# First inputs of a two-block network on one core: stage 0 of the parameter rows loaded and turned ahead of the others, x turned and split by quarters, its squares summed per token on ScalarE

## The reference

```python
hn = rmsnorm(h, norm_mix_g)            # y = x * rsqrt(mean(x*x) + eps), times the gain
proj = hn @ w_in + b_in                # 2048 x 13320
(q, k, v, o_pre, i_pre, f_pre, cb, cc, ch, gm_pre, gc_pre) = split(proj)
hm = mlstm_chunkwise(q, k, v, i_pre, f_pre)      # four heads, gates from i_pre, f_pre
```

## Time and profile before

| | us |
|---|---|
| three timed runs, median | 2799.66 |
| lowest, highest | 2789.32, 2804.08 |
| the profiled execution, its time | 2790.9 |
| its span (first to last instruction) | 2789.0 |
| TensorE busy in it | 2721.1 |
| VectorE, ScalarE busy | 1709.8, 1296.5 |

### The profile page before, as it was taken

One profiled execution on the slowest core, in us unless ns is written; L12 is line 12 of the kernel. 1 busy time (PEld: TensorE's weight loads), 2 busy tenths in 40 slices (PEclk: granted clock), 3 DMA queues, 4 the chain that ended last, 5 costly groups with the idle time before them and its releaser, 6 DMA issues.

```text
span 2789.0 us, 53028 instructions
## 1 busy us (share of the span) xinstructions
PE 2721.1 (98%) x22994; PEld 2703.2 (97%) x22994; DVE 1709.8 (61%) x1730; ACT 1296.5 (46%) x1448; POOL 1.8 (0%) x14
## 2 busy tenths in 40 slices
PE   4999999999999999999989999999999999999998
PEld 4899999999999999999989999999999999999998
DVE  4546464566667466746776687676665455554554
ACT  3445454445554344535553456664444344343343
POOL 0000000000000000000000000000000000000000
PEclk9999999999999999999999999999999999999999
DMA  4345555555555555555545555555555555555653
GB/s 157 123 152 182 192 190 191 195 193 186 188 191 180 196 181 189 188 193 177 182 144 182 169 180 182 191 187 194 194 187 182 191 187 183 184 192 185 189 185 108
DMA packets 257823, 503.31 MB, mean 180 GB/s; under 512 B 10151, under 2 KB 19039, under 8 KB 257631
## 3 DMA queue, kind: packets, MB, share of 16 engines
q1 hardware_dynamic: 254592, 500.20, 54.6%
q10 hardware_dynamic: 3054, 0.55, 0.1%
HBM read 498.63 MB, written 2.10 MB: 180 GB/s over the span
## 4 chain that ended last, share of the span: by engine, by line
PE 92%; DVE 4%; ACT 2%; ACTq 1%; issue 1%; DVEq 0%
PE psum L514 28%; PE psum L515 28%; PE psum L516 28%; PE psum L541 2%; PE psum L542 2%; PE psum L543 2%; DVE wlo L1233 1%; DVE work L1261 1%; ACTq L817 1%; ACT whi L831 1%; DVE hn L1271 0%; ACT hn L852 0%; PE psum L489 0%; PE psum L732 0%; PE psum L734 0%
## 5 line engine op out<-in xcount | busy, mean ns | idle before, releaser
L1233 DVE TENSOR_TENSOR wlo<-raw,whi 128x1024 fp32r<-128x1024 f32 x952 | 1160.8, 1223 | 968.7 <-ACT whi L831 965.9
L831 ACT ACTIVATE whi<-raw 128x1024 fp32r<-128x1024 f32 x952 | 1004.2, 1058 | 1293.4 <-PE psum L516 1180.9
L514 PE MATMUL psum<-hn,whi 128*128 128x256 f32 x4448 | 1247.4, 280 | 14.6 <-DVE wlo L1233 14.5
L515 PE MATMUL psum<-hn,whi 128*128 128x256 f32 x4448 | 1244.5, 280 | 0.0
L516 PE MATMUL psum<-hn,wlo 128*128 128x256 f32 x4448 | 1244.4, 280 | 0.0
L514 PEld LDWEIGHTS psum<-hn,whi 128*128 128x128 f32 x4448 | 848.1, 191 | 19.3 <-issue 10.1
L515 PEld LDWEIGHTS psum<-hn,whi 128*128 128x128 f32 x4448 | 841.1, 189 | 0.1
L516 PEld LDWEIGHTS psum<-hn,wlo 128*128 128x128 f32 x4448 | 839.3, 189 | 0.0
L514 PE MATMUL psum<-act,whi 128*128 128x256 f32 x2544 | 711.8, 280 | 13.2 <-DVE wlo L1233 9.7
L516 PE MATMUL psum<-act,wlo 128*128 128x256 f32 x2544 | 711.1, 280 | 0.0
L515 PE MATMUL psum<-act,whi 128*128 128x256 f32 x2544 | 711.1, 280 | 0.0
(11 more groups left out here) (214 smaller groups left out, 962.9 us busy)
## 6 DMA issues: line engine op xcount, KB each, us to landing
raw<-in_w_in SPq DMA_DIRECT2D x160, 1024.0 KB, 5.1
raw<-in_mlp_w SPq DMA_DIRECT2D x128, 1024.0 KB, 5.2
raw<-in_w_up SPq DMA_DIRECT2D x80, 1024.0 KB, 5.0
raw<-in_w_down SPq DMA_DIRECT2D x40, 1024.0 KB, 5.0
raw<-in_w_out SPq DMA_DIRECT2D x32, 1024.0 KB, 5.1
raw<-in_w_branch_m SPq DMA_DIRECT2D x8, 1024.0 KB, 5.0
raw<-in_w_branch_c SPq DMA_DIRECT2D x8, 1024.0 KB, 5.0
raw<-in_w_up SPq DMA_DIRECT2D x8, 768.0 KB, 4.3
```

The lines of the kernel that those rows point to most:

```text
L514: mm(o, hi[:, kk, w], both[:, 0, :], start=first and m % 2 == 0, stop=False)
L515: mm(o, hi[:, kk, w], both[:, 1, :], start=False, stop=False)
L831: A(whi[:, n % SLOTS, :], raw[:, n // 2 % RAW, n % 2 * HALF:(n % 2 + 1) * HALF], ACT.Copy)\
L1233: V.tensor_tensor(wlo[:, n % SLOTS, :], raw[:, n // 2 % RAW, n % 2 * HALF:(n % 2 + 1) * HALF], whi[:, n % SLOTS, :].bitcast(F32), ALU.subt ...
```

## The change

1. Stage 0 (norm_mix_g, b_in, mlstm_head_g, norm_ffn_g) is loaded by ScalarE first, then meta, wif, gate_b. The other five stages are loaded by SyncE, behind chunk 3.
2. TensorE turns x quarter 0, stage 0, x quarter 1, and starts group 0. Quarters 2 and 3 are turned at steps 0 and 2, inside the stream, in banks 2, 3 and 6, 7.
3. Squares: ScalarE squares x_nat, tokens on partitions, with an accumulated sum for each token (two instructions per quarter); VectorE adds the four quarters; TensorE spreads the totals over partitions with two 128-column matmuls at step 4. The squares of h, VectorE's reductions and norm_total(0) go.
4. Splits: two with quarter 0, two with quarter 1, none with 2 and 3; split 3 of the stream's step 0 goes. 
5. The meta tokens, gate logits, the other stages, softplus and the chain of the gates move to later steps: logits (PE) at 5, turn_rest at 8, copy_rest (DVE) at 10, softplus at 18, f_moved 9 (was 6), f_copied 11 (was 8), m_ready 12 (was 9), TensorE's wait for it 13 (was 10), decay 15 to 17 (was 12 to 14), scores 19 and 22 (was 18 and 21), st_made 21 and 24 (was 20 and 23), den 25 (was 24).

```diff
@@ SyncE
                             load_group(ph, i, i, s)
+                            if ph.name == "qkvo" and i == 0 and s == 0:
+                                for later in range(1, len(STAGES)):
+                                    load_stage(sp, later, "stage_loaded")
@@ stream
-                        if not isinstance(i, int) or not last_of_all(ph, i, AHEAD + s * n + k):
+                        if isinstance(i, int) and 2 * ph.c0 + 2 * n * i + s * n + k == 0:
+                            pass
+                        elif not isinstance(i, int) or not last_of_all(ph, i, AHEAD + s * n + k):
                             split(ph, i, AHEAD + s * n + k)
@@ TensorE
+            def turn_x(q):
+
+                pe.wait_ge(sem(f"x_loaded_{q}"), 16)
+                if q >= 2:
+                    pe.wait_ge(sem("x_copied"), 2 * q - 2)
+                for b in range(2):
+                    for f in range(2):
+                        for t in range(2):
+                            last = nc.tensor.transpose(psum[:, (2, 6)[q % 2] + b, f * T + t * P:f * T + (t + 1) * P],
+                                                       x_nat[:, t, (4 * q + 2 * b + f) * P:(4 * q + 2 * b + f + 1) * P],
+                                                       ident[:, :])
+                    last.then_inc(sem("x_turned"), 1)
...
             pe.wait_ge(sem("consts_ready"), 3)
-            for b in range(4):
-                turn_x(b)
-
-            pe.wait_ge(sem("stage_loaded"), STAGE_DMAS * 16)
...
+            turn_x(0)
+            pe.wait_ge(sem("first_stage_loaded"), len(STAGES[0]) * 16)
+            turn_stage(0, 4, 0).then_inc(sem("first_cols_turned"), 1)
+            turn_x(1)
...
-            def setup_sums():
-
-                pe.wait_ge(psum_freed, 2)
-                norm_total(0)
-
+            def spread_total():
+
+                pe.wait_ge(sem("token_total"), 1)
+                pe.wait_ge(sem("x_copied"), 6)
+                for t in range(2):
+                    last = mm(psum[:, 2, t * P:(t + 1) * P], token_total[:, t:t + 1].to_broadcast([P, P]), ident[:, :],
+                              start=True, stop=True)
+                last.then_inc(sem("norm_total"), 1)
+
+            def gate_logits():
+
+                pe.wait_ge(sem("gates_scaled"), 1)
+                pe.wait_ge(sem("x_copied"), 8)
...
+            def turn_rest():
+
+                pe.wait_ge(sem("stage_loaded"), STAGE_DMAS * 16)
+                for s in range(1, 5):
+                    turn_stage(s, 7, (s - 1) * P)
+                turn_stage(5, 6, 0)
                 pe.wait_ge(sem("meta_normed"), 1)
...
-                if x == MIDDLE:
-                    setup_sums()
-                elif x == 6:
+                if x == 0:
+                    turn_x(2)
+                elif x == 2:
+                    turn_x(3)
+                elif x == 4:
+                    spread_total()
+                elif x == 5:
+                    gate_logits()
+                elif x == 8:
+                    turn_rest()
+                elif x == 9:
                     pe.wait_ge(sem("logits_made"), 1)
...
-                elif x == 10:
+                elif x == 13:
+                    pe.wait_ge(sem("cols_copied"), 1)
                     pe.wait_ge(sem("m_ready"), 1)
@@ ScalarE
+            load_stage(ac, 0, "first_stage_loaded")
             ac.dma_start(meta_nat, a["meta_tokens_2"]).then_inc(sem("meta_loaded"), 16)
-            for s, rws in enumerate(STAGES):
...
             ac.dma_start(wif, by_tiles(a["w_in"])[:, :, GATE_COL:GATE_COL + 8]).then_inc(sem("gates_loaded"), 16)
...
+            def token_squares(q):
+
+                ac.wait_ge(sem(f"x_loaded_{q}"), 16)
+                if q:
+                    ac.wait_ge(sem("token_sum"), 2 * q)
+                for t in range(2):
+                    A(view(work, 6160 + 512 * t, 1, 512).rearrange("p a b -> p (a b)"),
+                      x_nat[:, t, q * 512:(q + 1) * 512], ACT.Square,
+                      accum_out=token_sums[:, t, q:q + 1]).then_inc(sem("token_sum"), 1)
...
             for q in range(4):
+                token_squares(q)
+                if q == 0:
+                    ac.wait_ge(sem("first_cols_copied"), 1)
                 ac.wait_ge(sem("x_copied"), 2 * q + 2)
                 high(q, lambda t: col("norm_mix_g", t))
-                if q < AHEAD:
-                    split(PH["qkvo"], 0, q)
-                square(q, q)
...
+                if q < 2:
+                    split(PH["qkvo"], 0, 2 * q)
+                    split(PH["qkvo"], 0, 2 * q + 1)
...
-                if x == MIDDLE + 1:
-                    root(0)
-                elif x == 8:
+                if x == 5:
+                    meta_root()
+                elif x == 6:
+                    ac.wait_ge(sem("norm_total"), 1)
+                    A(stream_scale, psum[:, 2, 0:T], ACT.Sqrt, bias=eps[:, 0:1], scale=1.0 / D)\
+                        .then_inc(sem("norm_root"), 1)
+                elif x == 12:
+                    ac.wait_ge(sem("cols_copied"), 1)
...
@@ VectorE
             for q in range(4):
...
+                copy_x(q)
+                if q == 0:
+                    ve.wait_ge(sem("first_cols_turned"), 1)
+                    nr = sum(n for _, n in STAGES[0])
+                    V.tensor_copy(cols[:, 0:nr], psum[:, 4, 0:nr]).then_inc(sem("first_cols_copied"), 1)
+                    ve.wait_ge(sem("first_cols_copied"), 1)
                     ve.sem_inc(psum_freed, 1)
+                    ve.wait_ge(sem("x_copied"), 2)
                 low_operand(0, q, lambda t: col("norm_mix_g", t))
-                if q < AHEAD:
-                    split(PH["qkvo"], 0, q)
-                sum_squares(q, q, squares, part)
-
+                if q < 2:
+                    split(PH["qkvo"], 0, 2 * q)
+                    split(PH["qkvo"], 0, 2 * q + 1)
+            ve.wait_ge(sem("token_sum"), 8)
+            V.tensor_reduce(token_total, token_sums, AX.X, ALU.add).then_inc(sem("token_total"), 1)
             ve.wait_ge(sem("gates_loaded"), 16)
...
-                setup_sums(x)
-                if x == 8:
+                if x == 6:
+                    first_root()
+                elif x == 7:
+                    scale_from_root(1)
+                elif x == 8:
+                    make_logits()
+                elif x == 10:
+                    copy_rest()
+                elif x == 18:
+                    softplus()
+                elif x == 11:
                     ve.wait_ge(sem("f_moved"), 1)
```

More of the change, by code:

```diff
@@ L163, in build @@
         part = view(work, 7184, 4, T)
+        token_sums, token_total = view(work, 7184, 2, 4), work[:, 7200:7202]
         squares2, part2 = view(work, 0, GW, T), view(work, 1024, 4, T)
@@ L260, in build, with rows, load_stage @@
         UP_FIRST = {"up_0": 0, "up_1": 16, "up_2": 32, "up_3": 40}
+        def rows(src, r):
+            return src.rearrange("(r p) -> r p", p=P)[0:r, :]
+        COLUMN_ROWS = {
+            "norm_mix_g": a["norm_mix_g"], "b_in_a": a["b_in"][0:GATE_COL], "b_in_b": a["b_in"][GATE_COL + 8:],
+            "mlstm_head_g": a["mlstm_head_g"], "norm_ffn_g": a["norm_ffn_g"], "ffn_conv_b": a["ffn_conv_b"],
+            "norm_out_g": a["norm_out_g"], "ffn_w0": a["ffn_conv_w"][0], "ffn_w1": a["ffn_conv_w"][1],
+            "ffn_w2": a["ffn_conv_w"][2], "norm1_g_2": a["norm1_g_2"][0], "pool_scale_2": a["pool_scale_2"][0],
+            "conv_b_2": a["conv_b_2"][0], "norm2_g_2": a["norm2_g_2"][0], "lru_lambda_2": a["lru_lambda_2"][0],
+            "final_g_2": a["final_g_2"],
+            "conv_w": a["conv_w"].rearrange("k (r p) -> (k r) p", p=P),
+            "conv_w_2": a["conv_w_2"][0].rearrange("k (r p) -> (k r) p", p=P),
+            "gate_a_b_2": a["gate_a_b_2"][0].rearrange("h (r p) -> (h r) p", p=P),
+            "gate_x_b_2": a["gate_x_b_2"][0].rearrange("h (r p) -> (h r) p", p=P),
+        }
+        def load_stage(eng, s, done):
+            at = 0
+            for name, n in STAGES[s]:
+                src = COLUMN_ROWS[name]
+                if len(src.shape) == 1:
+                    src = rows(src, n)
+                eng.dma_start(stage[at:at + n, s, :], src).then_inc(sem(done), 16)
+                at += n
         block = ctx.enter_context(nc.Block())
@@ L458, in spread_row, with turn_stage @@
                 return ident[0:HEADS, hd:hd + 1].to_broadcast([HEADS, P])
[L460 to L467, removed]
-            pe.wait_ge(sem("consts_ready"), 3)
-            for b in range(4):
-                turn_x(b)
-            pe.wait_ge(sem("stage_loaded"), STAGE_DMAS * 16)
[L474 to L482, removed]
+            def turn_x(q):
[9 more added lines that the diff above has]
+                    last.then_inc(sem("x_turned"), 1)
+            def turn_stage(s, bank, at):
+                nr = sum(n for _, n in STAGES[s])
+                return nc.tensor.transpose(psum[:, bank, at:at + nr], stage[0:nr, s, :], ident[0:nr, 0:nr])
```

(13 more changed lines are left out.)

163 lines of the change are left out of this document (80 added, 83 removed).

## The result

In twenty runs of each kernel the changed one takes 2770.95 us (2753.49 to 2794.17), the one before 2793.48 us (2782.67 to 2825.2): ratio 0.9924, 95% interval 0.9903 to 0.9945, so 15 to 27 us less, 22.5 by the medians. Forecast were 2772 and 24 us. Single runs of one kernel lie up to 40 us apart, so that the median came within about 1 us of the forecast is in part luck.

What follows compares the result with a forecast made beforehand. TensorE's long matmul stream bounds the kernel, so time is won only where it idles or clocks low. 20.7 to half-chunk 4 plus 3 at m_ready, about 24 us, off 2796 gives 2772; range 2757 to 2786.

Steps and rivals of the forecast that it cites:

- The list and its hold: ScalarE's start: list of 8 loads, gate_b held 8.6 us behind wif, first operand at about 16 us against 30.71.
- The prediction's second estimate: ScalarE's start: wif's 2048 pieces pass in 11 us, hold ends between 12 and 17 us, gain 0 to 4 less.
- First matmul: Start of TensorE's stream: 4.8 us behind the first operand, at 20.8 instead of 35.48, 14.7 us won.
- The walk to half-chunk 4: First operand to half-chunk 4: 24.5 us through ScalarE, VectorE and TensorE, with a 3 to 3.5 us wait for split 4.
- Work left behind it: TensorE after half-chunk 4's start: totals 0.4, logits 7.1, meta 1.2, five stage transposes 0.6, 9.3 us in all.
- The clock behind the wait: Half-chunk 4: the wait before it probably lets the clock fall once, costing 2.4 us, so 23.1 won becomes 20.7.
- m_ready: TensorE's wait in qkvo, moved from step 10 to 13: 3.5 instead of 5.6 us; 3 won, bounds -1 and 6.
- Sum at the marker: Whole gain: 20.7 us up to half-chunk 4 plus 3 at the m_ready wait, 23.7, called 24.
- Rival D: Early stream: clock stays low until past the logits, losing 17 us; gain 7, 2789 us; chance 10%.
- E: Clock stays low until the m_ready wait at step 13, costing 19 more; 12 us slower, 2808; chance 3%.
- C: ScalarE's start: gate_b held till bulk loads are nearly in, 18 to 25.8 us; gain 19 to 11, 2777 to 2785; 15%.
- F: Earlier start given back in TensorE waits for m_ready's chain or weight loads; within 0.5%, 2790 us; chance 4%.

Runs made afterwards that it cites:

- swap_gate_b: Changed kernel with ScalarE issuing gate_b ahead of wif; the marker (start of the factor products at the end of qkvo) came 4.1 us earlier.
- u_list: Changed kernel with all 23 small loads issued by ScalarE again, stage 0 first; first operand 14.6 us later, factor products at the end of qkvo 13.9 later.
- u_ahead: Changed kernel with x quarters 2 and 3 turned ahead of group 0; half-chunk 4 came 0.4 us later, factor products at the end of qkvo 1.1 earlier.
- u_squares: Changed kernel with squares of h, VectorE's reductions and four full products back; half-chunk 4 came 6.3 us later, factor products at the end of qkvo 5.0 later.
- the repeats: Both kernels profiled again, unedited; factor products at the end of qkvo at 215.7, 218.1, 218.2 us before and 191.7, 191.5, 191.4 changed.

## Why the prediction was right

**The list and its hold.** Forecast 8.6 us of hold and the first operand at 16; 7.46 and 14.33. Taking twice the 4.3 us hold of a 43 KB load was a guess between bounds 20 us apart, and it was near; that is luck in so far as no run shows that a hold grows with the load ahead of it. swap_gate_b shows that gate_b is held behind wif, as the prediction said, and u_list that the list passes nearly one to one to the marker. The prediction's second estimate let the hold last for as long as wif's pieces take to pass, until 12 to 17; it ended at 11.77, and the pieces were still passing. The Trainium skill's rule behind it (DMA: Bandwidth & Descriptors, Queues, rings and completion order), that a DMA engine takes turns between its queues, agrees with this trace: from 12 to 14 us the two queues moved 354 packets each. What failed in that estimate is taking the passage for the hold.

**First matmul.** 4.8 behind the first operand, as taken over: 19.10 - 14.33 = 4.8. Squares 0.6 and 0.2 each as taken, but they overlap: the pair took 1.24 (13.09 to 14.33) and not 1.6.

**The walk to half-chunk 4.** Forecast 24.5 behind the first operand, with a wait of 3 to 3.5 for split 4 behind high(3) and low(3); measured 37.85 - 14.33 = 23.5, wait 3.46. Half of the 1 us is the 0.5 allowed for a low clock in half 1. By the pace of its matmuls (0.21 us apart up to 23.5, 0.12 from 23.65 on) the clock rose just before half 0 was over; the clock column reads 1.00 all through this stretch, as it did in the first row. The other half is a link that the walk had wrong: it hung the last copies on TensorE's transposes of quarter 3, and they hung on VectorE's low(2). u_ahead and u_squares confirm which engines carry this walk.

**Work left behind it.** Forecast 9.3; logits 7.07, the rest in the chain's rows 0.5 for five stages and 1.1 for meta, and the spread totals 0.85. The last was mis-sized by a factor of two: they ran at the lower clock. The stage loads on SyncE's queue cost nothing, as forecast: TensorE waits nowhere for them.

**The clock behind the wait.** Forecast 2.4. Half-chunks 4 and 5 and the totals took 46.83 - 37.85 = 9.0 where two at 2.7 and 0.4 would be 5.8: 3.2. The low level outlasted half-chunk 4 and took in the totals.

**m_ready.** Forecast 5.6 to 3.5; measured 3.2. But the low clock did not get shorter as hoped. Before, it lasted about 7.5 us from the end of the wait at 98.6, here 10 us from the end of the wait at 81.8 (before, then after):

```profile
98.60:106.00 7.40, 7.37 (x26) 6.15 (x27) 2.71 (x3) 1.36 (x2) 0.00 (x0) 0.50 0.45 142
```

```profile
81.80:91.70 9.90, 9.90 (x38) 8.68 (x39) 2.57 (x3) 1.81 (x3) 0.00 (x0) 0.50 0.52 183
```

That took back about half of the 2.4 that the shorter wait won. 2 to 4 were forecast, about 1.3 came: this is the term of the sum that was most mis-sized.

**Sum at the marker.** 72.94 - 37.85 = 35.1, less 9.3 and 3.2, is 22.6, and half-chunk 10 says nearly the same (90.12 - 67.37 = 22.75); with 1.3, 24.0. Forecast 20.7 and 3. The parts were off by up to 2 us each, in both directions, so that their sum is right to 0.3 is luck; the repeats put it at up to 26.8. The baseline was taken 2.5 too high as well (2796, the median of twenty is 2793.48). The pieces of the chances add to 0.78 and 0.19, where 0.80 and 0.17 were given.

**Rival D** fell: the clock rose in the first half-chunk and eight transposes in the stream took 1.04, at the upper level. They neither kept it down nor dropped it. The Trainium skill's rule on transposes (TensorE: Matmul & The Clock Gate, Part 4: PE-mode transpose) is not contradicted by this, since matmuls of the stream stood around them, but it decides nothing here. The prediction's sign for D and E, a low clock beyond 30 us, did appear (0.50 from 40 to 43), as the dip behind the wait that the forecast itself counted on; as a sign it was ill chosen. E, C and F didn't occur.

**What stayed undivided.** u_list and u_squares give 14 and 5 to 6 of the 24 to 27. The m_ready wait gave 1.3 behind half-chunk 10. What remains, some 3 to 7, should lie in the meta squares and second table load moved off the start (3.5 between 27.20 and 30.71 in the earlier trace rows, less the 1.2 of the token squares put there) and in two splits with each quarter. That is read from the rows, not shown: I did not take these apart, nor try the two undone together.

## What to carry to other kernels

This kernel is 98% busy on one engine, and yet at its start the other engines set the time. There it pays to follow the chain through the feeding engines, not the busy one: taking four reductions off VectorE gave 5 to 6 us, starting TensorE 4 us earlier gave nothing. Ask of every load an engine issues ahead of its own work what is queued behind it; here a load in tiny pieces belongs last on the list (4.1 us). A wait of 3 us cost twice, once itself and once in the lower clock behind it: 2.3 and 2.7 us of waiting taken away gave 4.6 and about 5.8. And read such a gain where it arises: at a marker further on, each of the two edits also showed 1 to 3 us from the clock in a place that it doesn't touch.

## What the runs showed of the hardware

- An issue behind a load of 2048 pieces of 32 bytes is held: 7.46 us while bulk loads run, 4.69 as they end, 0.39 when it goes first. The hold of 7.46 was over long before those pieces had passed (about 550 of 2048 started, the load landed 9.5 us later).
- While both queues had work, SyncE's and ScalarE's moved 354 packets each from 12 to 14 us, though SyncE's came to 0.69 MB and ScalarE's to 0.01.
- The time at the lower clock behind one and the same wait (m_ready, 3.2 and 3.3 us) differed: from 81.8 to 91.7 in the changed kernel, from 79.4 to 82.6 with splits 4 and 5 behind quarter 2, worth 3.1 us.
- TensorE's stream has two paces at the same granted clock: 884 or 852 matmuls per 100 us, 113 or 117 ns each. In the profiles taken here a loop keeps the pace with which it begins, and the same program shows both from run to run. One loop of some 340 us is worth about 13 us (the lead of 24.0 at the marker is 10.9 behind it), so a few such loops could make up much of the scatter of 40 us between runs of one kernel; with three profiles of each that is not shown. What sets it I don't know; no run here was made to find out. To compare versions of this kernel, read a marker ahead of the loops, or take many runs.
